# Rounding and subtracting the weights of a decoder layer in halves of eight k-tiles instead of quarters of four

## The chip, the cores and the metric

The kernel runs on one core of a Trainium2 chip. The metric is the device time of one execution in microseconds (us), shown as the median of three runs. One further execution was taken by the hardware profiler; all durations below are from it.

## What is computed

One layer of a decoder, for a prompt of 272 positions (16 learned tokens and 256 of the prompt) and for 64 sampled positions (8 requests of 8). Cut to what matters here:

```python
z = rmsnorm(x) @ w_in                    # split into q, k, v, indexer, conv, gate_A, gate_B
A = sparse_attend(q, k, v, top_k(index_scores(...))) @ w_attn_br
B = silu(layernorm(causal_conv(glu(cz)))) @ w_conv_br
h = x + (sigmoid(gate_A) * A + sigmoid(gate_B) * B) @ w_out
y = h + (silu(rmsnorm(h) @ w_gate) * (rmsnorm(h) @ w_up)) @ w_down
```

All of it is float32. The sampled positions read keys and values of 1024 earlier positions from a paged cache.

## The kernel before, in words

**Strips.** Every weight matrix goes through one pipeline, in strips of 128 output columns. A strip has 16 k-tiles of 128x128 (the fourth part of the feed-forward's last stretch, `dn2`, multiplies 12). SyncE loads a strip into one of four buffers, `RAW[:, s]`. ScalarE rounds it to the matmul's type, `WH` (two buffers, `s % 2`). VectorE writes the remainder `WL = RAW - WH` over `RAW`. TensorE makes three matmuls for each k-tile, `XH*WH + XL*WH + XH*WL` (L1355 to L1357), 48 for a strip, into the PSUM tile `G[s % 2]`; then VectorE or ScalarE reads it out.

**Who works for which strip.** While TensorE multiplies strip s, ScalarE and VectorE prepare strip s+2: `ahead` does a whole strip, `ahead_quarter` one piece of it at a time, between other work. Until now a piece is a quarter, 4 k-tiles. ScalarE's quarter r of strip s+2 overwrites the WH buffer of strip s, so it waits on `mm_done` until TensorE has multiplied quarter r of strip s (L535); VectorE's waits for ScalarE's on `hi_done` (L900); TensorE's matmuls wait on `lo_done`.

**The stage cz.** The GLU columns (16 strips, four loop passes of four) are multiplied while the paged keys come in. TensorE runs, for each quarter j of a strip (L1647 to L1671): eight transposes of one page of keys (`kst`) into PSUM, the 12 matmuls of the weight quarter j, and, on every second page, the 32 instructions of the scores `psS<-kTs,qsz` (16 matmuls in the code), which wait until both halves of that page have been copied from PSUM to `kTs`. ScalarE copies one half (L722) and VectorE the other (L1126); right after its copy number j, each calls `ahead_quarter(..., j)`. VectorE also has a top-k step (L1019 or L1023) behind its copies 0 and 2. So on both engines a copy and a weight piece alternate in one queue, and the order in which they stand there is the order of the code.

**Other stages that the prediction speaks of.** `qk` and `v` (projections, with `ahead`); the prompt's attention, which starts when VectorE has copied the last values; `ga` and `gbA` (gates), where VectorE alternates `ahead_quarter` with the depthwise convolution (L1205 and lines near it) and, at piece 14 of gbA's 16, makes `OL` (L1237), which the next stage's first matmul needs; `out`, whose last sum of squares TensorE takes at the end; and the three parts of the feed-forward, `gu` and `dn`.

Of the kernel before, what the change touches and what calls it, by code (L numbers as in the profile page):

```python
# [24 lines left out]
F32 = mybir.dt.float32  # L25
F32R = mybir.dt.float32r
I32 = mybir.dt.int32
ALU = mybir.AluOpType
ACT = mybir.ActivationFunctionType
# [12 lines left out]
IH, ID = 16, 64  # L42
# [184 lines left out]
def layer(nc, I, O):  # L227
# [34 lines left out]
    XH, XL, RAW, WH, WL = T["XH"], T["XL"], T["RAW"], T["WH"], T["WL"]  # L262
# [17 lines left out]
    nothing = zer[:, 0:4 * IH].rearrange("p (k n) -> p k n", k=4)  # L280
# [7 lines left out]
    with ExitStack() as ctx:  # L288
        G, TB, SB, MB = ([ctx.enter_context(nc.psum_tensor(f"ps{n}{i}", [P, 512], F32)) for i in range(2)] for n in "GTSM")

        def sem(name):
            return ctx.enter_context(nc.semaphore(name))
# [6 lines left out]
        hi_done, lo_done, mm_done = sem("hi_done"), sem("lo_done"), sem("mm_done")  # L299
# [225 lines left out]
        def _(act):  # L525
            ch = Chain(act, act_ch)

            def hi(G_, s, first=False):
                act.wait_ge(w_ld[s], 32 * G_ + 32)
                for r in range(4):  # L530
                    quarter(G_, s, r, first)

            def quarter(G_, s, r, first=False):
                if not first:
                    act.wait_ge(mm_done, 16 * G_ + (4 * s + r - 7))  # L535
                if isinstance(G_, int) and G_ == G0["ikiw"]:
                    if s:
                        act.activation(WH[:, s % 2, 4 * r:4 * r + 4, 0:IH], nothing, ACT.Copy).then_inc(hi_done, 1)
                        return
                    c = slice(0, ID + IH)  # L540
                else:
                    c = slice(0, P)
                act.activation(WH[:, s % 2, 4 * r:4 * r + 4, c], RAW[:, s, 4 * r:4 * r + 4, c], ACT.Copy).then_inc(hi_done, 1)  # L543

            def ahead(G_, s, last=False):
                if not (last and s >= 2):
# [2 lines left out]
            def ahead_quarter(G_, s, r):  # L549
                G_, s = G_ + (s + 2) // 4, (s + 2) % 4  # L550
                if r == 0:
                    act.wait_ge(w_ld[s], 32 * G_ + 32)
                quarter(G_, s, r)
# [62 lines left out]
            for i in range(2):  # L616
                c = slice(half * i, half * i + half)
                act.activation(ikT[0:ID, c], MB[0][0:ID, c], ACT.Copy).then_inc(ev[i], 1)
            for i in range(2):
                c = slice(half * i, half * i + half)  # L620
# [78 lines left out]
            for h in range(H):  # L699
                slot, c = h // 2 % 2, slice(P * (h % 2), P * (h % 2) + P)  # L700
# [188 lines left out]
        def _(dve):  # L889
# [4 lines left out]
            def lo(G_, s):  # L894
                for r in range(4):
                    quarter(G_, s, r)

            def quarter(G_, s, r):
                k = slice(4 * r, 4 * r + 4)
                dve.wait_ge(hi_done, 16 * G_ + (4 * s + r + 1))  # L900
                if isinstance(G_, int) and G_ == G0["ikiw"]:
                    if s:
                        dve.tensor_copy(WL[:, s, k, 0:IH], nothing).then_inc(lo_done, 1)
                        return
                    c = slice(0, ID + IH)
                else:
                    c = slice(0, P)
                dve.tensor_tensor(WL[:, s, k, c], RAW[:, s, k, c], WH[:, s % 2, k, c].bitcast(F32), ALU.subtract).then_inc(lo_done, 1)  # L908

            def ahead(G_, s, last=False):  # L910
                if not (last and s >= 2):
# [2 lines left out]
            def ahead_quarter(G_, s, r):  # L914
                quarter(G_ + (s + 2) // 4, (s + 2) % 4, r)
# [324 lines left out]
            for u in range(4 * GN["wa"]):  # L1240
                G_, s = G0["wa"] + u // 4, u % 4
# [32 lines left out]
            for u in range(4 * GN["wc"]):  # L1274
                G_, s, f = G0["wc"] + u // 4, u % 4, 2 * u
# [610 lines left out]
```

## Time and profile before

| | |
|---|---|
| median of three runs | 2174.16 us (2171.81 to 2174.58) |
| the profiled execution's own time | 2179.28 us |
| its span in the trace | 2177.8 us |
| TensorE (PE) matmuls | busy 2085.5 us, 96% of the span |
| VectorE (DVE) | busy 1235.7 us, 57% |
| ScalarE (ACT) | busy 902.6 us, 41% |
[...]

Busy time of TensorE is modelled from pipelined matmuls, so consecutive matmuls overlap in it: the distance between their starts tells the pace. "Idle before" is the time an engine waited ahead of an instruction, with what it waited for. [...]

### The profile page before, as it was taken

Reading aid. Unit: us, or ns where it says so; the run is one execution under the profiler, and the core shown is the slowest. Engines: PE = TensorE matmul, PEld = TensorE weight load, DVE = VectorE, ACT = ScalarE, POOL = GpSimd, SP = SyncE. Lnnn points to the kernel's source line nnn. Section 1 sums busy time; section 2 is a strip of 40 time slices with the busy share of each in tenths; the row PEclk is TensorE's granted clock in tenths of the full one; section 3 lists DMA queues with packets and bytes.
Section 4 is the critical chain, followed back from the end, with each engine's and each line's share of the span. In section 5 each row is a group of like instructions: output and inputs, shape, how many; then the busy total and the mean of one; then the engine's idle time right before and its main releaser. Section 6 shows DMA issues by size and latency. Waiting matters only on the chain.

```text
span 2177.8 us, 40501 instructions
## 1 busy us (share of the span) xinstructions
PE 2085.5 (96%) x14573; PEld 1970.8 (90%) x14573; DVE 1235.7 (57%) x2261; ACT 902.6 (41%) x1647; POOL 158.5 (7%) x286
## 2 busy tenths in 40 slices
PE   6969999979998999999999999999999999999997
PEld 5945999769997777999999999999999999999997
DVE  5324988526666799874664455554455544455553
ACT  6423443334444333436444454543344443344443
POOL 5300000011112121000000000000000000000012
PEclk9988999679998999999999999999999999999999
DMA  9450456237786798455654455555555555555574
GB/s 237 93 120 20 117 134 169 65 127 241 242 241 208 243 320 279 133 148 134 193 148 135 135 152 145 147 154 152 144 149 154 153 143 147 154 153 144 147 205 114
DMA packets 545493, 350.55 MB, mean 161 GB/s; under 512 B 15122, under 2 KB 524346, under 8 KB 545007
## 3 DMA queue, kind: packets, MB, share of 16 engines
q1 hardware_dynamic: 518480, 263.55, 44.9%
q0 software_dynamic: 25824, 84.55, 12.1%
q8 instruction: 70, 1.15, 0.2%
q10 hardware_dynamic: 1088, 1.05, 0.1%
q14 instruction: 31, 0.25, 0.0%
HBM read 338.91 MB, written 10.83 MB: 161 GB/s over the span
## 4 chain that ended last, share of the span: by engine, by line
PE 67%; DVE 1%; ACT 0%; issue 0%; POOL 0%; DVEq 0%; POOLq 0%; ACTq 0%
PE psG L1355 20%; PE psG L1356 20%; PE psG L1357 20%; PE psS L1352 2%; PE psM L1355 1%; PE psM L1356 1%; PE psM L1357 1%; PE psM L1352 1%; PE psM L1349 0%; PE psG L1349 0%; DVE stat L1178 0%; PE psT L1349 0%; DVE OL L1237 0%; ACT L L744 0%; PE psS L1349 0%
## 5 line engine op out<-in xcount | busy, mean ns | idle before, releaser
L908 DVE TENSOR_TENSOR WL<-RAW,WH 128x512 fp32r<-128x512 f32 (+1 forms) x996 | 672.6, 689 | 684.2 <-ACT WH L543 683.1
L543 ACT ACTIVATE WH<-RAW 128x512 fp32r<-128x512 f32 (+1 forms) x996 | 617.3, 629 | 886.7 <-PE psG L1357 827.2
L1355 PE MATMUL psG<-XH,WH 128*128 128x320 f32 (+1 forms) x2688 | 852.1, 317 | 19.7 <-ACT iwT L621 16.7
L1356 PE MATMUL psG<-XL,WH 128*128 128x320 f32 (+1 forms) x2688 | 841.8, 313 | 0.0
L1357 PE MATMUL psG<-XH,WL 128*128 128x320 f32 (+1 forms) x2688 | 839.6, 312 | 0.0
L1355 PEld LDWEIGHTS psG<-XH,WH 128*128 128x128 f32 x2688 | 510.3, 190 | 51.2 <-issue 30.9
L1356 PEld LDWEIGHTS psG<-XL,WH 128*128 128x128 f32 x2688 | 510.3, 190 | 1.1
L1357 PEld LDWEIGHTS psG<-XH,WL 128*128 128x128 f32 x2688 | 510.7, 190 | 0.0
L1355 PE MATMUL psG<-MH,WH 128*128 128x320 f32 x960 | 301.2, 314 | 0.3 <-DVE ML L1324 0.3
L1357 PE MATMUL psG<-MH,WL 128*128 128x320 f32 x960 | 296.6, 309 | 0.0
L1356 PE MATMUL psG<-ML,WH 128*128 128x320 f32 x960 | 296.5, 309 | 0.0
L1355 PEld LDWEIGHTS psG<-MH,WH 128*128 128x128 f32 x960 | 180.5, 188 | 1.6 <-issue 0.5
L1356 PEld LDWEIGHTS psG<-ML,WH 128*128 128x128 f32 x960 | 180.5, 188 | 1.1
L1357 PEld LDWEIGHTS psG<-MH,WL 128*128 128x128 f32 x960 | 180.4, 188 | 0.0
L1205 DVE SCALAR_TENSOR_TENSOR ya<-ub,wdw,ya 128x256 f32<-128x256 f32 x232 | 100.2, 479 | 0.0
L514 POOL DMA_DIRECT2D out<-ytok x16 | 11.5, 720 | 1101.7 <-ACT ytok L868 1097.7
L1349 PE MATMUL psT<-ident,kst 128*128 128x128 f32 x512 | 68.9, 278 | 6.2 <-DMA kst<-in_cache_k 6.2
L1349 PEld LDWEIGHTS psT<-ident,kst 128*128 128x128 f32 x512 | 58.0, 142 | 13.0 <-issue 12.5
L1126 DVE COPY kTs<-psT 128x512 f32<-128x512 f32 x64 | 43.9, 686 | 43.0 <-PE psT L1349 43.0
L722 ACT ACTIVATE kTs<-psT 128x512 f32<-128x512 f32 x64 | 38.2, 597 | 46.8 <-PE psT L1349 46.5
L858 ACT ACTIVATE MH<-at 128x320 f32 x44 | 20.8, 472 | 82.8 <-DVE at L1322 82.8
L480 POOL DMA_DIRECT2D kst<-in_cache_k x64 | 33.8, 529 | 176.7 <-issue 176.7
(347 smaller groups left out, 1729.7 us busy)
## 6 DMA issues: line engine op xcount, KB each, us to landing
RAW<-in_w_in SPq DMA_DIRECT2D x160, 512.0 KB, 5.2
RAW<-in_w_ffn_down SPq DMA_DIRECT2D x96, 512.0 KB, 5.0
RAW<-in_w_ffn_gate SPq DMA_DIRECT2D x88, 512.0 KB, 4.9
RAW<-in_w_ffn_up SPq DMA_DIRECT2D x88, 512.0 KB, 4.6
kst<-in_cache_k POOLq DMA_DIRECT2D x64, 512.0 KB, 4.5
vst<-in_cache_v POOLq DMA_DIRECT2D x64, 512.0 KB, 5.8
RAW<-in_w_out SPq DMA_DIRECT2D x32, 512.0 KB, 4.8
RAW<-in_w_attn_br SPq DMA_DIRECT2D x16, 512.0 KB, 4.7
```

Of the source, the lines that this page charges most:

```text
L480: pool.dma_start(dst[:, n:n + 1, :], src[bass.ds(page(g * m + n, ptab2), 1)].rearrange("o s n -> s o n")).then_inc(landed[n], 16)
L543: act.activation(WH[:, s % 2, 4 * r:4 * r + 4, c], RAW[:, s, 4 * r:4 * r + 4, c], ACT.Copy).then_inc(hi_done, 1)
L722: act.activation(kTs[:, j % 2, 0:4, :], TB[0][:].rearrange("p (h n) -> p h n", h=4), ACT.Copy).then_inc(kc_A, 1)
L858: act.activation(MH[:, bass.ds(g * 2 + s // 2, 1), :], at2[:, s // 2:s // 2 + 1, :], ACT.Copy).then_inc(ah_dn, 1)
L908: dve.tensor_tensor(WL[:, s, k, c], RAW[:, s, k, c], WH[:, s % 2, k, c].bitcast(F32), ALU.subtract).then_inc(lo_done, 1)
L1126: dve.tensor_copy(kTs[:, j % 2, 4:8, :], TB[1][:].rearrange("p (h n) -> p h n", h=4)).then_inc(kc_D, 1)
L1205: ch.step(dve.scalar_tensor_tensor(z, x, tap, z, ALU.mult, ALU.add))
L1349: return pe.transpose(out, src, ident[0:n, 0:n])
L1352: return pe.matmul(out, lhsT, rhs, start=start, stop=stop, skip_group_check=True)
L1355: pe.matmul(out, WH[:, s % 2, k], hi, start=start, stop=False)
L1356: pe.matmul(out, WH[:, s % 2, k], lo, start=False, stop=False)
L1357: return pe.matmul(out, WL[:, s, k], hi, start=False, stop=stop)
```

## The change

The pieces in which ScalarE rounds and VectorE subtracts become halves of 8 k-tiles. The calls stay where they were; those for odd pieces return at once. The call for piece 0 now does k-tiles 0 to 7 and waits for TensorE's quarters 0 and 1 of strip s; that for piece 2 does k-tiles 8 to 15 and waits for quarters 2 and 3. The counts on `hi_done` and `lo_done` go up by two at a time; TensorE's waits, the loads and all other work are as before.

```diff
@@ ScalarE @@
             def quarter(G_, s, r, first=False):
+                if r % 2:
+                    return
                 if not first:
-                    act.wait_ge(mm_done, 16 * G_ + (4 * s + r - 7))
+                    act.wait_ge(mm_done, 16 * G_ + (4 * s + r - 6))
...
-                act.activation(WH[:, s % 2, 4 * r:4 * r + 4, c], RAW[:, s, 4 * r:4 * r + 4, c], ACT.Copy).then_inc(hi_done, 1)
+                act.activation(WH[:, s % 2, 4 * r:4 * r + 8, c], RAW[:, s, 4 * r:4 * r + 8, c], ACT.Copy).then_inc(hi_done, 2)
@@ VectorE @@
             def quarter(G_, s, r):
-                k = slice(4 * r, 4 * r + 4)
-                dve.wait_ge(hi_done, 16 * G_ + (4 * s + r + 1))
+                if r % 2:
+                    return
+                k = slice(4 * r, 4 * r + 8)
+                dve.wait_ge(hi_done, 16 * G_ + (4 * s + r + 2))
...
-                dve.tensor_tensor(WL[:, s, k, c], RAW[:, s, k, c], WH[:, s % 2, k, c].bitcast(F32), ALU.subtract).then_inc(lo_done, 1)
+                dve.tensor_tensor(WL[:, s, k, c], RAW[:, s, k, c], WH[:, s % 2, k, c].bitcast(F32), ALU.subtract).then_inc(lo_done, 2)
```

ScalarE in the stage cz, from the first copy of a strip on (`kTs<-psT` is the copy of a page's half, `WH<-RAW` the rounding; names in brackets are the semaphores waited for). Before:

```order
L722 ACTIVATE kTs<-psT 128x512 [waits k_tr]
L552 ISA
L535 ISA [waits w_ld2]
L543 ACTIVATE WH<-RAW 128x512 [waits mm_done]
L721 REGISTER_ALU
L722 ACTIVATE kTs<-psT 128x512 [waits k_tr]
L535 REGISTER_ALU
L543 ACTIVATE WH<-RAW 128x512 [waits mm_done]
```

and with the change:

```order
L724 ACTIVATE kTs<-psT 128x512 [waits k_tr]
L554 ISA
L537 ISA [waits w_ld2]
L545 ACTIVATE WH<-RAW 128x1024 [waits mm_done]
L723 REGISTER_ALU
L724 ACTIVATE kTs<-psT 128x512 [waits k_tr]
L723 REGISTER_ALU
L724 ACTIVATE kTs<-psT 128x512 [waits k_tr]
```

The rounding of 1024 elements stands where that of 512 stood, between copy 0 and copy 1; behind copy 1 there is none any more. The order of the copies is the same, the `mm_done` that the rounding waits for is one quarter later.

VectorE in the same place (`WL<-RAW,WH` is the subtraction, `MAX` and `MATCH_REPLACE` the top-k step). Before:

```order
L1126 COPY kTs<-psT 128x512 [waits k_tr]
L104 ISA
L108 MEMSET stat 1x1 [waits dve_ch]
L1019 MAX m8s<-Ws 64x8
L900 ISA
L908 TENSOR_TENSOR WL<-RAW,WH 128x512 [waits hi_done]
L1125 REGISTER_ALU
L1126 COPY kTs<-psT 128x512 [waits k_tr]
L900 REGISTER_ALU
L908 TENSOR_TENSOR WL<-RAW,WH 128x512 [waits hi_done]
```

and with the change:

```order
L1130 COPY kTs<-psT 128x512 [waits k_tr]
L104 ISA
L108 MEMSET stat 1x1 [waits dve_ch]
L1023 MAX m8s<-Ws 64x8
L904 ISA
L912 TENSOR_TENSOR WL<-RAW,WH 128x1024 [waits hi_done]
L1129 REGISTER_ALU
L1130 COPY kTs<-psT 128x512 [waits k_tr]
L1129 REGISTER_ALU
L1130 COPY kTs<-psT 128x512 [waits k_tr]
```

As on ScalarE: copy 1 now stands behind a subtraction of a whole half.

VectorE at the end of gbA (`OL<-oT,OH` is the operand of the next stage's first matmuls, `ya` the convolution). Before:

```order
L908 TENSOR_TENSOR WL<-RAW,WH 128x512 [waits hi_done]
L1205 SCALAR_TENSOR_TENSOR ya<-ub,wdw,ya 128x256 [waits dve_ch]
L908 TENSOR_TENSOR WL<-RAW,WH 128x512 [waits hi_done]
L1237 TENSOR_TENSOR OL<-oT,OH 128x2560 [waits oh_dn]
L1205 SCALAR_TENSOR_TENSOR ya<-ub,wdw,ya 128x256 [waits dve_ch] x2
L908 TENSOR_TENSOR WL<-RAW,WH 128x512 [waits hi_done]
```

and with the change:

```order
L912 TENSOR_TENSOR WL<-RAW,WH 128x1024 [waits hi_done]
L1209 SCALAR_TENSOR_TENSOR ya<-ub,wdw,ya 128x256 [waits dve_ch] x2
L912 TENSOR_TENSOR WL<-RAW,WH 128x1024 [waits hi_done]
L1241 TENSOR_TENSOR OL<-oT,OH 128x2560 [waits oh_dn]
L1209 SCALAR_TENSOR_TENSOR ya<-ub,wdw,ya 128x256 [waits dve_ch] x3
L912 TENSOR_TENSOR WL<-RAW,WH 128x1024 [waits hi_done]
```

Before, one quarter of the strip came behind OL; now the whole strip's preparation comes ahead of it.

## Rows read from the trace of the kernel before

**Rows 1.** The page's busy time: us, share of the span, instructions.

```profile
PE 2085.5 (96%) x14573; PEld 1970.8 (90%) x14573; DVE 1235.7 (57%) x2261; ACT 902.6 (41%) x1647; POOL 158.5 (7%) x286
```

**Rows 2.** Stretches: us, busy (count) of PE, PEld, DVE, ACT, POOL; clock, DMA share, GB/s.

```profile
520.00:700.00 180.00, 173.46 (x1854) 160.62 (x1846) 112.37 (x205) 77.64 (x122) 30.34 (x58) 0.98 0.76 232
...
760.00:860.00 100.00, 100.00 (x687) 76.57 (x686) 92.66 (x183) 32.28 (x68) 20.71 (x39) 1.00 0.99 316
...
1500.00:1800.00 300.00, 300.00 (x2053) 300.00 (x2052) 148.81 (x247) 119.64 (x203) 0.00 (x0) 1.00 0.55 150
```

**Rows 3.** Groups of instructions by line and shape: count, busy us, mean ns, idle before.

```profile
L908 DVE TENSOR_TENSOR WL<-RAW,WH 128x512 fp32r<-128x512 f32 x992 | 670.7, 690 | 680.6 <-ACT WH L543 679.5 <-DVE rf L1306 0.2
L543 ACT ACTIVATE WH<-RAW 128x512 fp32r<-128x512 f32 x992 | 615.5, 629 | 883.0 <-PE psG L1357 823.5 <-PE psM L1357 28.8 <-DMA RAW<-in_w_in 14.3
...
L1237 DVE TENSOR_TENSOR OL<-oT,OH 128x2560 fp32r<-128x2560 f32 x1 | 2.8, 2819 | 0.0
...
L584 ACT ACTIVATE ikb<-ikst 128x1024 f32<-128x1024 f32 x8 | 8.5, 1061 | 0.2
```

**Rows 4.** Timeline of one page in cz: start us, us, engine, line, instruction, idle before.

```profile
569.61 1.04 PE L1349 MATMUL psT<-ident,kst 128*128 128x128 f32 x8
...
570.47 0.69 DVE L908 TENSOR_TENSOR WL<-RAW,WH 128x512 fp32r<-128x512 f32 x1 [0.68 <-ACT WH L543]
...
571.08 0.68 DVE L1126 COPY kTs<-psT 128x512 f32<-128x512 f32 x1
...
572.18 0.31 PE L1357 MATMUL psG<-XH,WL 128*128 128x336 f32 x1
572.42 1.08 PE L1352 MATMUL psS<-kTs,qsz 128*32 128x128 f32 x32
572.53 0.63 ACT L543 ACTIVATE WH<-RAW 128x512 fp32r<-128x512 f32 x1 [1.25 <-PE psG L1357]
573.19 0.69 DVE L908 TENSOR_TENSOR WL<-RAW,WH 128x512 fp32r<-128x512 f32 x1 [1.43 <-ACT WH L543]
```

**Rows 5.** Timeline at the end of gbA, around OL.

```profile
898.34 2.82 DVE L1237 TENSOR_TENSOR OL<-oT,OH 128x2560 fp32r<-128x2560 f32 x1
...
898.83 0.63 ACT L543 ACTIVATE WH<-RAW 128x512 fp32r<-128x512 f32 x1 [1.13 <-PE psG L1357]
...
901.30 0.38 PE L1355 MATMUL psG<-OH,WH 128*128 128x320 f32 x1 [2.52 <-DVE OL L1237]
```

**Rows 6.** What TensorE waited for: line, whom; us in total, times, longest.

```profile
PE psT L1352 <- DVE vs L1064: 2.2, 1, 2.2
PE psG L1355 <- DVE WL L908: 2.1, 1, 2.1
PE psM L1352 <- ACT sq L648: 2.0, 4, 0.5
PE psM L1352 <- ACT sq L840: 1.9, 1, 1.9
PE psM L1349 <- DVE L L1146: 1.8, 1, 1.8
...
PE psG L1355 <- DVE ML L1324: 0.3, 1, 0.3
```

**Rows 7.** Stretches behind four of TensorE's waits (columns as in rows 2).

```profile
36.00:40.00 4.00, 4.00 (x19) 4.00 (x18) 3.53 (x6) 2.12 (x5) 1.43 (x3) 0.57 1.01 353
...
689.00:692.00 3.00, 2.89 (x14) 1.98 (x12) 1.02 (x2) 1.84 (x4) 1.49 (x3) 0.55 0.88 259
900.00:904.00 4.00, 2.70 (x18) 2.73 (x19) 2.95 (x5) 0.60 (x1) 0.00 (x0) 1.00 0.94 257
1232.00:1236.00 4.00, 4.00 (x21) 4.00 (x21) 2.84 (x2) 2.26 (x3) 0.00 (x0) 0.70 0.07 18
```

**Rows 8.** Timeline of TensorE in the first of these stretches: matmuls 1 and 12.

```profile
36.48 0.47 PE L1355 MATMUL psG<-XH,WH 128*128 128x320 f32 x1
...
39.42 0.47 PE L1357 MATMUL psG<-XH,WL 128*128 128x320 f32 x1
```

More of the change, by code:

```diff
@@ L533, in quarter @@
             def quarter(G_, s, r, first=False):
+                if r % 2:
+                    return
                 if not first:
-                    act.wait_ge(mm_done, 16 * G_ + (4 * s + r - 7))
+                    act.wait_ge(mm_done, 16 * G_ + (4 * s + r - 6))
                 if isinstance(G_, int) and G_ == G0["ikiw"]:
                     if s:
-                        act.activation(WH[:, s % 2, 4 * r:4 * r + 4, 0:IH], nothing, ACT.Copy).then_inc(hi_done, 1)
+                        act.activation(WH[:, s % 2, 4 * r:4 * r + 4, 0:IH], nothing, ACT.Copy).then_inc(hi_done, 2)
                         return
@@ L898, in quarter @@
             def quarter(G_, s, r):
-                k = slice(4 * r, 4 * r + 4)
-                dve.wait_ge(hi_done, 16 * G_ + (4 * s + r + 1))
+                if r % 2:
+                    return
+                k = slice(4 * r, 4 * r + 8)
+                dve.wait_ge(hi_done, 16 * G_ + (4 * s + r + 2))
                 if isinstance(G_, int) and G_ == G0["ikiw"]:
                     if s:
-                        dve.tensor_copy(WL[:, s, k, 0:IH], nothing).then_inc(lo_done, 1)
+                        dve.tensor_copy(WL[:, s, 4 * r:4 * r + 4, 0:IH], nothing).then_inc(lo_done, 2)
                         return
```

## The prediction

> **What bounds the kernel now.** I read the page's busy times first, then the stretches, the groups of instructions by line, and the timeline of one page in the stage cz. TensorE is busy for 96% of the span [rows 1], and in the long weight stages it never stops: 2053 matmuls in 300 us, one every 0.146 us, at clock 1.00 [rows 2], so that a strip of 48 takes 7.0 us. ScalarE's rounding and VectorE's subtraction spend more time waiting than working: 883 us of idle ahead of 616 us of work, nearly all of it for TensorE's matmuls, and 681 us ahead of 671 us, nearly all of it for ScalarE [rows 3]. They are early, not late. So a saving on them is worth nothing by itself, and the question is where a later or longer piece makes TensorE wait.
>
> **What a piece costs.** A quarter takes 629 ns on ScalarE and 690 ns on VectorE [rows 3]. The halves have 1024 elements instead of 512. For ScalarE the group of ikb, a copy of 128x1024, shows 1061 ns: I take 1.06 us, 0.43 more than a quarter. For VectorE the subtraction of 2560 elements took 2819 ns [rows 3]; the line through 512 and 2560 gives 690 + 512 x (2819 - 690) / 2048 = 1222 ns, 0.53 more than a quarter. Two quarters cost 1258 and 1380 ns, so a strip saves 0.4 us on ScalarE and 0.3 us on VectorE, in time that they now spend waiting.
>
> **Steady strips: nothing.** The second half can start when TensorE ends strip s and is finished 1.06 + 1.22 us later, some 2.3 us; it is needed in the middle of strip s+2, 7.0 + 3.5 us later. PSUM is read out up to 0.96 us later than now, some 3 us after a strip's end, and needed again 7.0 us after it. That covers both.
>
> **The stage cz: a new wait on every second page.** Now, ScalarE's piece j waits for TensorE's quarter j, and while it is done TensorE is at the eight transposes and the matmuls of the next page; both copies of that page are finished long before TensorE asks for them. The timeline shows it: transposes from 569.61, VectorE's subtraction at 570.47, its copy at 571.08 to 571.76, TensorE's last matmul of the quarter at 572.18, and its scores at 572.42 without a wait [rows 4]. With the change piece 0 stands between copy 0 and copy 1, as before, but waits for TensorE's quarter 1, and that quarter is done only when TensorE stands in front of the scores that need copy 1. Copy 1 sits behind that piece on both engines. The same holds for piece 2 and copy 3. It is no deadlock, since quarter 1 doesn't need copy 1, but from then on everything is in series:
> - ScalarE starts at 572.53, as now [rows 4], and takes 1.06: 573.59.
> - VectorE starts 0.03 us after ScalarE's end (573.19 against 572.53 + 0.63 [rows 4]): 573.62. It takes 1.22: 574.84.
> - Its copy starts 0.08 us before the subtraction's shown end (571.08 against 570.47 + 0.69) and takes 0.68 [rows 4]: 574.76 to 575.44. ScalarE's own copy is ready sooner.
> - TensorE starts 0.14 us after VectorE's end (901.30 against 898.34 + 2.82 [rows 5]): 575.58.
>
> Against 572.42 that is 3.16 us of standstill, with nothing else for TensorE to do, since its instructions stand in order too. Two in each of 16 strips: 32 x 3.16 = **101 us**. What could be off by some tenths is each hand-over; I keep 2.9 and 3.4 us (93 and 109 us) as ends.
>
> [...]
>
> **The clock in cz.** Waits of this length have let TensorE's clock fall. Of four in the trace, 2.1 us for WL, 1.8 us for L, 1.9 us for sq at L840 [rows 6] and 2.5 us for OL [rows 5], the stretches behind the first three show a granted clock of 0.57, 0.55 and 0.70, the one behind OL 1.00 [rows 7]. [...] Between the two I take 1.25 us: 32 x 1.25 = **40 us**. The ends are nothing (the clock holds, as behind OL) and 60 us, if some of the slow stretches last longer than the one measured.
>
> **Single places where TensorE already waits for a piece or for what is behind one.** There the longer piece is paid in full, 0.43 us if only ScalarE's is in the chain and 0.96 us if both are:
> - at the start, for the first WL (2.1 us now): 0.96;
> - at the end of each pass of qk, for sq at L648 (four times, 0.5 each): 4 x 0.43 = 1.7;
> - at the start of the prompt's attention, for vs (2.2): 0.96;
> - at the end of out, for sq at L840 (1.9): 0.96;
> - at the start of the last dn, for ML (0.3): 0.96 [rows 6].
> - OL: it now starts at 898.34, behind a quarter that was ready early; with the change it comes behind the whole second half, which starts only at 898.83 [rows 5]: 898.83 + 1.06 + 0.03 + 1.22 - 0.08 = 901.06, so 2.7 us later, and TensorE waits 5.2 us instead of 2.5.
> - The end of cz: two quarters (0.63 + 0.69) are gone from behind TensorE's last quarter, ahead of the last logits; the last standstill has 1.3 us of this in it: minus 1.3.
>
> Together 7 us; I keep 3 and 11 as ends.
>
> **Stage ga.** From 760 to 860 VectorE is busy for 92.7% and TensorE for all of it [rows 2]. Its pieces may run late by up to a strip before TensorE notices, and halves make its work a little less. I take nothing.
>
> **The sum.** 101 + 40 + 7 = 148 us on the profiled execution's own 2179.28 us, 2327 us. That execution lies 5.1 us above the median of the runs, 2174.16 us, so the forecast for the median is **2322 us**, slower by 6.8%.
>
> **The rivals.**
> - *The clock holds in cz.* For it: behind OL it did [rows 7]. Against: three of four. 2174.2 + 101 + 7 = 2282 us. This lies inside the forecast's mechanism and its range; I don't count it apart.
> - *The clock stays low through all of cz.* Each standstill could come before the clock has recovered from the one ahead. For it: in cz as it is there are 180 us with the clock at 0.98 [rows 2], all of which could be lost. [...] Against: behind the waits shown the lower clock ends within some us of steady matmuls, and cz has over 6 us of them between two standstills. 0.08.
> - *Only one standstill in a strip, or half of each.* It would be so if one of the two copies weren't behind its piece after all. 2174.2 + 50 + 20 + 7 = 2251 us. Against: the order of both queues, which is the same at pieces 0 and 2. 0.03.
> - *Faster.* The pieces' fixed cost is what counts, in ga, where VectorE is busy for 92.7% [rows 2]: if TensorE there waited for WL, the change would give back 2 x 690 - 1222 = 158 ns twice in each of 16 strips, 5 us, and 2169 us if cz had no standstill. It decides from the point where VectorE runs behind by a whole strip; TensorE's busy time of 100.00 in that stretch says that it doesn't, and the series in cz is against it. [...] 0.03.
> - *No change.* The copies in cz are finished before TensorE asks, say because the pieces don't wait where I read it. 2174 us; 0.02.
>
> **How the numbers follow.** The forecast has 0.84. Its low end is 93 + 0 + 3 us on the median, 2270 us; its high end 109 + 60 + 11 us, 2354 us. I let the range reach to 2370 us, where part of cz would run at the lower clock throughout; beyond it lies the second rival, below it the third to fifth, together 0.16. A measurement of this kernel can tell a difference of about 0.2%, 4 us, from none. Faster by more than that: 0.03; within it: 0.02; slower by more: 0.95.
>
> **What would show it.** Right: in cz, TensorE's first scores instruction of every second page waits about 3.2 us for VectorE's kTs copy, 32 times, some 100 us in the list of waits; the pieces there stand in the timeline directly behind the last matmul of an odd quarter, with the copy directly behind the subtraction; half the pieces on both engines, of about 1.06 and 1.22 us; a granted clock well below 0.98 in cz; the wait for OL at 5.2 us. Wrong: if TensorE's idle time in cz stays small, the order isn't what I think; if the waits are there and the clock stays at 1.00, only the clock's term falls; if the kernel after cz takes clearly longer than before, I have missed a place.

## The result, and the profile after

The changed kernel takes **2362.8 us** (median of four runs, 2360.87 to 2364.72), the kernel before 2173.84 us beside it: a ratio of 1.0871 (1.0852 to 1.0890), 189 us more. The profiled execution took 2360.87 us, 181.6 us more than the profiled one of before (2179.28 us, which lies some 5 us above its median).

The page of the changed kernel, its busy times (columns as in [rows 1]):

```profile
PE 2153.2 (91%) x14573; PEld 2030.0 (86%) x14573; DVE 1179.7 (50%) x1757; ACT 814.6 (35%) x1143; POOL 159.0 (7%) x286
```

VectorE and ScalarE have 504 instructions less each and 56 and 88 us less to do. TensorE has the same 14573 matmuls and its share falls from 96% to 91%, because it now waits. Its granted clock in tenths of full speed, by slices of 59 us and from the same page, shows where:

```profile
PEclk9989998687777769999999999999999999999999
```

Slices 9 to 14 are from 472 to 826 us, most of the stage cz: one 8 and five times 7. What TensorE waited for, the rows that answer to [rows 6] and the new ones (line, whom; us in total, times, longest):

```profile
PE psS L1356 <- DVE kTs L1130: 83.9, 26, 3.2
PE psS L1356 <- issue: 19.1, 6, 3.2
...
PE psG L1359 <- DVE OL L1241: 5.4, 1, 5.4
...
PE psM L1356 <- ACT sq L650: 3.9, 4, 1.0
...
PE psG L1359 <- DVE SGA L1251: 3.4, 2, 1.7
...
PE psG L1359 <- DVE WL L912: 3.0, 1, 3.0
PE psM L1356 <- ACT sq L842: 3.0, 1, 3.0
PE psT L1356 <- DVE vs L1068: 2.8, 1, 2.8
...
PE psG L1359 <- DVE ML L1328: 1.4, 1, 1.4
```

The first two rows are new: 26 + 6 = 32 waits, 103.0 us in all, 3.2 us each, always ahead of the scores of a second page. ("issue" is the same wait where the profile saw no releaser.) The pieces themselves, groups by line and shape, answer to [rows 3]:

```profile
L912 DVE TENSOR_TENSOR WL<-RAW,WH 128x1024 fp32r<-128x1024 f32 x496 | 605.6, 1224 | 828.6 <-ACT WH L545 828.0 <-DVE Wp L1015 0.4
L545 ACT ACTIVATE WH<-RAW 128x1024 fp32r<-128x1024 f32 x496 | 523.9, 1059 | 972.4 <-PE psG L1361 914.5 <-PE psM L1361 32.6 <-issue 15.6
```

Half as many, of 1224 and 1059 ns, and both engines wait longer than before: what the larger pieces saved went into waiting.

The series itself, in the timeline of one page in cz (start us, us, engine, line, instruction, idle before), where [rows 4] had no wait:

```profile
622.31 0.31 PE L1361 MATMUL psG<-XH,WL 128*128 128x336 f32 x1
622.72 1.06 ACT L545 ACTIVATE WH<-RAW 128x1024 fp32r<-128x1024 f32 x1 [4.85 <-PE psG L1361]
...
623.88 1.23 DVE L912 TENSOR_TENSOR WL<-RAW,WH 128x1024 fp32r<-128x1024 f32 x1 [4.77 <-ACT WH L545]
625.02 0.68 DVE L1130 COPY kTs<-psT 128x512 f32<-128x512 f32 x1
...
625.80 1.93 PE L1356 MATMUL psS<-kTs,qsz 128*32 128x128 f32 x32 [3.18 <-issue]
...
627.67 1.78 PE L1353 MATMUL psT<-ident,kst 128*128 128x128 f32 x8
```

TensorE's last matmul of the quarter ends at 622.62; only then does ScalarE's rounding start, then the subtraction, then the copy, then the scores. And the scores take 1.93 us where they took 1.08: the standstill is followed by a slower clock, which is the other part of the loss.

Stretches of TensorE's clock, the columns of [rows 2] and the same two windows of 180 and 300 us, then the whole of cz:

```profile
520.00:700.00 180.00, 131.73 (x1083) 122.06 (x1082) 59.86 (x94) 38.82 (x53) 15.90 (x30) 0.78 0.43 130
...
1500.00:1800.00 300.00, 300.00 (x2049) 300.00 (x2048) 134.25 (x154) 115.88 (x123) 0.00 (x0) 1.00 0.54 148
...
476.00:852.00 376.00, 273.33 (x2265) 253.25 (x2263) 126.86 (x200) 80.64 (x111) 31.84 (x60) 0.80 0.43 130
```

In the same 180 us there are 1083 matmuls instead of 1854, at a granted clock of 0.78 instead of 0.98. (Before, cz ended at 686 us in this window: its part of it had a clock of 1.00, and the missing 0.02 belong to what comes behind cz.) In 300 us of the feed-forward there are 2049 against 2053, at 1.00: that stage noticed nothing. The kTs copies in cz begin at 474.0 and 683.6 us before, at 476.1 and 851.5 us now (first and last), so the stage went from 209.6 to 375.4 us. **165.8 of the 181.6 us are here**: 103.0 of standstill, and 62.8 that are left for the clock. The other 15.8 us lie outside cz.

### The profile page after: what moved, and what is told of

The parts are those of the page before. It is cut to its first block, busy times and chain, and to the rows that moved or that the text cites. A ratio compares the mean times of both kernels' runs of the same rounds, so it can differ in the third digit from the quotient of the medians.

```text
span 2359.4 us, 39696 instructions
## 1 busy us (share of the span) xinstructions
PE 2153.2 (91%) x14573; PEld 2030.0 (86%) x14573; DVE 1179.7 (50%) x1757; ACT 814.6 (35%) x1143; POOL 159.0 (7%) x286
## 4 chain that ended last, share of the span: by engine, by line
PE 61%; DVE 1%; ACT 1%; issue 0%; POOL 0%; DVEq 0%; POOLq 0%; ACTq 0%
PE psG L1359 19%; PE psG L1360 19%; PE psG L1361 19%; PE psS L1356 2%; PE psM L1360 1%; PE psM L1359 1%; PE psM L1356 1%; PE psM L1361 1%; ACT WH L545 0%; PE psM L1353 0%; DVE ub L1214 0%; DVE yp L1218 0%; PE psG L1353 0%; DVE stat L1182 0%; DVE WL L912 0%
## 5 line engine op out<-in xcount | busy, mean ns | idle before, releaser
L912 DVE TENSOR_TENSOR WL<-RAW,WH 128x1024 fp32r<-128x1024 f32 (+1 forms) x498 | 607.2, 1223 | 832.2 <-ACT WH L545 831.6
L1359 PE MATMUL psG<-XH,WH 128*128 128x320 f32 (+1 forms) x2688 | 860.9, 320 | 23.4 <-ACT iwT L623 17.7
L545 ACT ACTIVATE WH<-RAW 128x1024 fp32r<-128x1024 f32 (+1 forms) x498 | 525.4, 1057 | 976.2 <-PE psG L1361 918.3
L1359 PEld LDWEIGHTS psG<-XH,WH 128*128 128x128 f32 x2688 | 516.9, 192 | 55.0 <-issue 33.6
L1360 PEld LDWEIGHTS psG<-XL,WH 128*128 128x128 f32 x2688 | 516.2, 192 | 1.4 <-issue 0.4
L1356 PE MATMUL psS<-kTs,qsz 128*32 128x128 f32 x1024 | 60.6, 413 | 103.0 <-DVE kTs L1130 83.9
L1356 PEld LDWEIGHTS psS<-kTs,qsz 128*32 128x32 f32 x1024 | 47.2, 164 | 110.9 <-issue 110.9
L1353 PE MATMUL psT<-ident,kst 128*128 128x128 f32 x512 | 92.0, 340 | 6.0 <-DMA kst<-in_cache_k 6.0
L1353 PEld LDWEIGHTS psT<-ident,kst 128*128 128x128 f32 x512 | 78.7, 180 | 18.3 <-issue 17.9
```

Of the source, the lines that this page charges most:

```text
L545: act.activation(WH[:, s % 2, 4 * r:4 * r + 8, c], RAW[:, s, 4 * r:4 * r + 8, c], ACT.Copy).then_inc(hi_done, 2)
L1353: return pe.transpose(out, src, ident[0:n, 0:n])
L1356: return pe.matmul(out, lhsT, rhs, start=start, stop=stop, skip_group_check=True)
L1359: pe.matmul(out, WH[:, s % 2, k], hi, start=start, stop=False)
L1360: pe.matmul(out, WH[:, s % 2, k], lo, start=False, stop=False)
```

## The experiments

Theory: the 32 standstills come from the order in the two queues (the piece behind copy 0 waits for TensorE's next quarter, copy 1 stands behind the piece), and the low clock comes from the standstills. Rivals: the size of the pieces as such is what costs, the low clock has a cause of its own in cz, or a good part of the loss lies outside cz. The first four runs shared a chip and nine runs of the kernel before (2172.51 us); the last four another chip and 21 runs of it (2172.59 us).

### Halves everywhere but in cz

ScalarE's and VectorE's old functions for a quarter are kept beside the new ones, under the name `fourth`, and cz calls them:

```diff
-                        ahead_quarter(G0["cz"] + g, s, j)
+                        ahead_fourth(G0["cz"] + g, s, j)
@@ VectorE @@
-                        ahead_quarter(G_, s, j)
+                        ahead_fourth(G_, s, j)
```

> Halves everywhere except in the stage cz, where the pieces are quarters again. Theory A (the order in cz: a half stands ahead of the copy that TensorE waits for, and its signal comes a quarter later): the 103 us of standstill and the low clock behind them are gone; cz is as long as before (210 us) and what is left is the small places outside cz, 10 to 16 us, so 2184 to 2190 us. Rival B (larger pieces cost wherever they are, by crowding the engines or the memory): most of the 189 us stays, over 2300 us.

Measured: 2190.98 us, ratio 1.0086 (1.0061 to 1.0112). The stretch of cz in this kernel:

```profile
474.00:685.00 211.00, 211.00 (x2267) 197.75 (x2265) 130.15 (x231) 89.77 (x142) 31.69 (x60) 1.00 0.74 230
```

Clock 1.00, TensorE busy throughout, no wait for kTs in the list, and cz 209.2 us long as before. So of 189 us about 171 belong to cz. What is left, 18.5 us, is well over the prediction's 7 us for the single places (3 to 11), and a little more than the 10 to 16 us that I expected of this run. Its list of waits has OL at 5.4 us and a row that the prediction doesn't name:

```profile
PE psG L1392 <- DVE OL L1274: 5.4, 1, 5.4
...
PE psG L1392 <- DVE SGA L1284: 3.4, 2, 1.7
```

### Quarters everywhere but in cz

The reverse: the kernel before, with halves in cz alone (`ahead_half` is the change's function under a name of its own).

```diff
-                        ahead_quarter(G0["cz"] + g, s, j)
+                        ahead_half(G0["cz"] + g, s, j)
@@ VectorE @@
-                        ahead_quarter(G_, s, j)
+                        ahead_half(G_, s, j)
```

> Quarters everywhere except in the stage cz, where the pieces are halves. Theory A: 32 waits of 3.2 us and a granted clock of about 0.8 in cz, 2174 + 166 = 2340 us (2335 to 2346). Rival B: only cz's share of the pieces (32 of 496 halves), so below 2200 us.

Measured: 2342.9 us, ratio 1.0782 (1.0734 to 1.0829). Its waits and its stretch of cz:

```profile
PE psS L1389 <- DVE kTs L1163: 83.9, 26, 3.2
PE psS L1389 <- issue: 19.1, 6, 3.2
...
PE psG L1392 <- DVE OL L1274: 2.5, 1, 2.5
```

```profile
471.00:845.00 374.00, 270.97 (x2266) 251.12 (x2269) 126.79 (x202) 80.00 (x111) 31.69 (x60) 0.80 0.43 130
```

The same 103.0 us and the same clock of 0.80; OL is back at 2.5 us. The two halves of the change add up: 170.4 + 18.5 = 188.9 us, against 189.0 measured for both together.

### The half called behind the odd copy

Halves everywhere as in the change, but in cz piece 0 is called behind copy 1 and piece 2 behind copy 3, so that no copy stands behind a piece that waits for the quarter in front of that copy's scores.

```diff
-                        ahead_quarter(G0["cz"] + g, s, j)
+                        if j % 2:
+                            ahead_quarter(G0["cz"] + g, s, j - 1)
@@ VectorE @@
-                        ahead_quarter(G_, s, j)
+                        if j % 2:
+                            ahead_quarter(G_, s, j - 1)
```

> Halves everywhere, but in cz both engines do piece 0 behind copy 1 and piece 2 behind copy 3, in place of behind copies 0 and 2. The size of the pieces and the signals they wait for stay the same. Theory A (place in the queue): nothing that TensorE waits for stands behind a waiting piece any longer; the 32 waits fall to less than 0.3 us each, the clock in cz is back above 0.97, and the time is that of cz in quarters, 2184 to 2196 us (VectorE has the logits of two pages to do behind piece 2, which may cost up to 5 us). Rival C (the later signal itself: the weights are prepared a quarter later and that is what TensorE feels): over 2300 us still.

Measured: 2199.09 us, ratio 1.0113 (1.0073 to 1.0153), 3 us above the upper end. The 32 waits of the scores are gone. What TensorE still waits for kTs, and the stretch of cz:

```profile
PE psT L1355 <- DVE kTs L1131: 3.5, 7, 0.5
```

```profile
476.00:690.00 214.00, 210.46 (x2251) 195.68 (x2251) 124.59 (x198) 82.23 (x109) 31.69 (x60) 0.99 0.74 227
```

The pieces are as large as in the change, and 164 of the 189 us are gone: size alone is not the cause, order is. The kernel takes 8.1 us more than with cz in quarters. Of these, 4.8 us are in cz: 3.5 us are waits of the transposes for a PSUM buffer that VectorE's copy releases, a copy that now stands behind a half. The other 1.3 us in cz and the 3.3 us outside it aren't assigned.

### The standstill filled with matmuls that lead to nothing

The change, with 20 matmuls of 128x320 put ahead of the scores of every second page. They write to PSUM that nobody reads and wait for nobody, so TensorE is active through the standstill; 640 more matmuls in all. (The first added line waits once, ahead of cz, until ScalarE has read out what stood in that PSUM tile.)

```diff
+            pe.wait_ge(sc_cp, CT)
...
+                        if n % 2:
+                            for _ in range(20):
+                                mm(MB[0][:, 0:NQ], XH[:, 0, 0:P], XH[:, 0, 0:NQ])
```

> The changed kernel with 20 matmuls of 128x320 that lead to nothing in each of the 32 standstills (ahead of the wait for copies 1 and 3), about 3 us each at the full clock; it computes nothing else than before. Theory D (64 of cz's 167 us are TensorE's lower clock behind the standstills): the waits themselves shrink to 0.2 to 0.4 us because the filling takes their place, cz is no shorter by that, but its clock goes to 0.97 or more and it loses about 60 us: 2300 us (2295 to 2312). Rival E (transposes and scores run slower for another reason, say the transfers of keys and weights beside them): no less than 2355 us.

Measured: **2297.38 us**, ratio 1.0574 (1.0534 to 1.0614): with 640 matmuls more, 65 us less than the changed kernel. Its waits for kTs, and its stretch of cz:

```profile
PE psS L1356 <- DVE kTs L1130: 7.9, 26, 0.3
...
PE psS L1356 <- issue: 1.6, 6, 0.3
```

```profile
478.00:792.00 314.00, 304.81 (x2897) 290.65 (x2895) 125.07 (x197) 80.20 (x110) 31.13 (x59) 1.00 0.50 153
```

The clock is 1.00 and every one of the scores takes 1.08 us. Cz is 105.9 us longer than before: the standstill of 103 us is all there, the clock's part is gone. So the low clock follows from TensorE standing still. Its price of 62.8 us, until now only what was left over, is measured by itself: 60 us between cz's first and last copy (375.4 to 315.5 us), 65 us by the medians of the two kernels.

### Quarters that wait as late as the halves

The kernel before, with quarter-sized pieces; in cz pieces 0 and 1 stand together behind copy 0 and wait for TensorE's quarter 1, as the half does (2 and 3 likewise).

```diff
-                        ahead_quarter(G0["cz"] + g, s, j)
+                        if j % 2 == 0:
+                            n_, t_ = G0["cz"] + g + (s + 2) // 4, (s + 2) % 4
+                            act.wait_ge(mm_done, 16 * n_ + (4 * t_ + j - 6))
+                            for r in (j, j + 1):
+                                ahead_quarter(G0["cz"] + g, s, r)
@@ VectorE @@
-                        ahead_quarter(G_, s, j)
+                        if j % 2 == 0:
+                            for r in (j, j + 1):
+                                ahead_quarter(G_, s, r)
```

> The kernel before with one difference in cz: behind copy 0 both engines do pieces 0 and 1, behind copy 2 pieces 2 and 3, still quarters of four k-tiles, and ScalarE first waits for the later signal, as the halves do. Theory A (the place and the signal, not the size of an instruction): the 32 standstills are there, shorter by what the two engines overlap. Quarters behind one another end at 0.66 + 0.61 + 0.69 = 1.96 us after TensorE's last matmul instead of 2.35 us, so 2.8 us each, 90 us, and on top 30 to 60 us of lower clock: 2290 to 2325 us. Rival F (the size of the piece): no more than 0.4 us each, below 2190 us.

Measured: 2299.37 us, ratio 1.0569 (1.0536 to 1.0603). Small pieces, and most of the loss is there: 126.8 of the 170.4 us that halves in cz alone cost come with the later signal. Its waits and its clock in cz:

```profile
PE psS L1358 <- DVE kTs L1130: 73.4, 26, 2.9
...
PE psS L1358 <- issue: 17.1, 6, 2.9
```

```profile
472.00:803.00 331.00, 241.62 (x2266) 223.88 (x2265) 128.21 (x231) 83.46 (x143) 31.70 (x60) 0.90 0.48 147
```

The wait is shorter, 90.5 us / 32 = 2.8 us, since VectorE begins the first quarter (at 606.85 us in one of them) while ScalarE does the second (both from 606.19 to 607.34). Cz is 121.2 us longer, so only 30.7 us are the clock's, half of the 62.8. So the size of the piece does count, by the length of the standstill: 12.5 us less of waiting, and with the shorter standstills 32.1 us less of lower clock. The timeline of TensorE shows where the clock's part went, in two standstills in a row:

```profile
608.85 1.94 PE L1358 MATMUL psS<-kTs,qsz 128*32 128x128 f32 x32 [2.85 <-issue]
...
619.80 1.08 PE L1358 MATMUL psS<-kTs,qsz 128*32 128x128 f32 x32 [2.82 <-DVE kTs L1130]
```

and the clock granted behind each:

```profile
608.85:612.16 3.31, 3.31 (x41) 2.93 (x41) 0.00 (x0) 0.00 (x0) 0.00 (x0) 0.53 0.00 0
619.80:622.60 2.80, 2.80 (x46) 2.60 (x47) 0.66 (x3) 0.60 (x1) 0.00 (x0) 1.00 1.17 313
```

Behind one wait of 2.8 us the granted clock is 0.53, behind the next, as long, 1.00. From 527 us on they alternate without exception; in all of cz the scores are slowed behind 17 of the 32 standstills (two of them in part), and behind the first only the transposes are, which makes 18. In the changed kernel, with 3.2 us, the scores are slowed behind 31 of 32 (one in part). A standstill with a slow clock behind it costs 30.7 / 18 = 1.7 us here and 62.8 / 31 = 2.0 us there: what differs most is how often it falls due.

### The gates in quarters as well

The first experiment, with quarters also in gbA and wa on both engines, and on ScalarE in gbB. This goes after the waits outside cz. (`ahead_fourths` calls `ahead_fourth` for all four quarters.)

```diff
-                ahead_quarter(G0["gbA"], n // 4, n % 4)
+                ahead_fourth(G0["gbA"], n // 4, n % 4)
@@ VectorE, wa @@
-                    ahead_quarter(G_, s, r)
+                    ahead_fourth(G_, s, r)
@@ ScalarE, gb (in wa the same) @@
-                ahead(G_, s)
+                ahead_fourths(G_, s)
```

> Quarters in cz, in the gates gbA (on ScalarE also in gbB) and in wa; halves elsewhere. What is tried is the cost of halves in gbA and wa, beside the kernel with only cz in quarters (2191.0 us). Theory G: the later OL (2.9 us of wait and 1.5 us of lower clock behind it) and the two waits for SGA in wa (3.4 us), which I had left out, are due to a whole half and two lots of convolution standing ahead of them: 7 to 8 us less, 2183 us, OL's wait back at 2.5 us and no wait for SGA. Rival H (convolution steps run late whatever the pieces): no change, 2191 us.

Measured: 2184.66 us, ratio 1.0055 (1.0033 to 1.0077), 6.3 us less than with cz alone in quarters. OL is back at 2.5 us and there is no wait for SGA:

```profile
PE psG L1396 <- DVE OL L1278: 2.5, 1, 2.5
```

2.9 us for OL and 3.4 for SGA are 6.3 us. That this fits to a tenth is luck: the theory had 1.5 us more, for the lower clock behind OL, and the runs of each of the two kernels spread over 4 to 5 us. The two sets of runs don't overlap (2180.24 to 2185.09 against 2189.19 to 2193.07).

### OL made earlier, in the first experiment and in the kernel before

With cz in quarters and halves elsewhere, OL is made at piece 9 of gbA instead of 14; then the same edit alone, in the kernel before.

```diff
-                if n == 14:
+                if n == 9:
                     dve.wait_ge(oh_dn, 1)
```

> As the kernel with only cz in quarters (2191.0 us), but VectorE makes OL five pieces earlier, behind piece 9 of gbA instead of piece 14. Theory G: the wait for OL (5.4 us) and the lower clock behind it (1.5 us) are gone; the waits for SGA stay, as they hang on the convolution steps: 2184 us. Rival I: OL's 2.8 us on VectorE only move, and TensorE waits somewhere else in wa as much longer: 2189 us or more.

Measured: 2183.57 us, ratio 1.0047 (1.0028 to 1.0066), 7.4 us less than with OL late. No wait for OL is left, and SGA's stays:

```profile
PE psG L1392 <- DVE SGA L1284: 3.4, 2, 1.7
```

The wait was 5.4 us. The other 2 us fit the clock that was lost behind it (at most 1.7 us, as the section below shows), but a difference of that size is not clear of the spread of the runs.

> The kernel before with OL made behind piece 9 of gbA instead of piece 14, nothing else. The wait of 2.5 us for OL is gone and no other comes: 2.5 us less than before, 0.1%, about what a measurement can just tell. Rival: VectorE is busy there and the convolution moves back: no change.

Measured: 2171.47 us (12 runs) against 2172.59, ratio 0.9998 (0.9978 to 1.0017). In the trace the wait of 2.5 us is gone, but 2.5 us are 0.1%, and the runs spread from 2158 to 2178 us: by time this is undecided. No version here is shown to beat the kernel before.

## Why the prediction was right, and where its sizes were off

The forecast was 2322 us, slower, with a range of 2270 to 2370; 2362.8 lies inside, 41 us above the point, and the mechanism is the one forecast. The sizes were less good: the upper ends of its own terms add up to 2354, and only the widening to 2370 holds the result. Of the 41 us, 23 are the clock in cz, 9 the single places and 2 the standstills; the other 7 are scatter, since the profiled execution of before lay 5 us above its median and that of the changed kernel 2 us below.

- **The standstills: right.** 32 were forecast at 3.16 us, 101 us; 32 came at 3.2, 103.0 us, at the place and in the order that the steps gave. With halves but no copy behind the late signal they are gone (half called later), with quarters behind the late signal they are there (late quarters): it is the signal and the queue that make them; the size only sets how long they last.
- **The clock in cz: the step that was mis-sized.** The prediction took 1.25 us a standstill, 40 us; it was 2.0 us, 63 us, above even its upper end of 60. No run shows the 1.25 us, a value that I chose between two estimates: twelve weight matmuls at the lower level behind WL, 0.267 us apart [rows 8] in place of 0.146, are 12 x 0.121 = 1.45 us, and three quarters of that are 1.1. The weighing was a little low: 31 of 32 had the lower clock, where three of four waits had shown it before [rows 7], and 1.45 us for each would have given 46 us. The larger part is the length. The cost of a fall was read from that one stretch, 3.2 us of weight matmuls. In cz the scores and eight transposes follow the standstill, and behind every second one the lower level lasts longer than that, into the weight matmuls:

```profile
613.40:616.90 3.50, 3.50 (x41) 3.12 (x41) 1.08 (x3) 0.00 (x0) 0.00 (x0) 0.50 0.88 229
616.90:622.60 5.70, 5.70 (x34) 5.43 (x32) 1.84 (x3) 0.60 (x1) 1.06 (x2) 0.82 0.32 92
625.80:629.20 3.40, 3.40 (x40) 3.02 (x41) 0.00 (x0) 0.00 (x0) 0.00 (x0) 0.51 0.00 0
629.20:634.00 4.80, 4.80 (x35) 4.55 (x33) 1.90 (x4) 0.60 (x1) 1.06 (x2) 1.00 0.35 108
```

  Two standstills in a row of the changed kernel, ended at 613.40 and 625.80: both have about 0.50 up to the end of the transposes; behind the first the weight matmuls run at 0.82, behind the second at 1.00. That is some 5.5 us at the lower level behind the first (3.5 us, and twice 0.18 x 5.7) and 3.4 us behind the second. What runs there matters little: the weight matmuls lost 0.121 of 0.267 us each, 45%, the scores lose 1.93 - 1.08 = 0.85 us, 44%, the transposes of the page shown 1.78 - 1.04 = 0.74 us, 42%. 45% of 5.5 and of 3.4 us are 2.5 and 1.5 us, 2.0 on average, the price that was measured. The prediction had this case, slow stretches longer than the one measured, as the end of its range and not as its point. Why the lower level lasts longer behind every second standstill is not shown.
- **Single places: 7 us forecast, 15.8 in the traces, 18.5 by the runs.** The waits that were named came out close: OL 5.4 (forecast 5.2), WL 3.0 (2.1 + 0.96), sq at the end of out 3.0 (1.9 + 0.96), vs 2.8 (2.2 + 0.96), ML 1.4 (0.3 + 0.96), and sq in qk 3.9 (2.0 + 1.7). The 1.3 us forecast as a gain at the end of cz didn't come: the stretch from cz's last scores to ga's first matmul is 1.2 us longer than before (28.9 against 27.7 us). The wait for the logits `L` there did fall, but only by 0.6 us, to 1.2, and the last scores alone lost 0.86 us to the clock. Two things were missed. One is the clock behind OL: it was 1.00 there before [rows 7], and now is 0.81 over the 9 us that follow,

```profile
1071.00:1080.00 9.00, 6.84 (x37) 6.87 (x38) 3.60 (x5) 1.06 (x1) 0.00 (x0) 0.81 0.23 60
```

  at most 9 x 0.19 = 1.7 us. The other is SGA, 3.4 us. In wa VectorE does its second half only when the strip has ended, and two lots of convolution then stand ahead of the two readings of PSUM that TensorE waits for, as the timeline of both engines there shows:

```profile
1090.15 1.23 DVE L912 TENSOR_TENSOR WL<-RAW,WH 128x1024 fp32r<-128x1024 f32 x1 [1.08 <-ACT WH L545]
1091.29 1.19 DVE L1218 TENSOR_TENSOR yp<-ub,wdw 128x992 f32<-128x992 f32 x1
...
1094.96 1.19 DVE L1214 TENSOR_REDUCE ub<-yp 128x32 f32<-128x992 f32 x1
...
1096.69 0.48 DVE L1250 TENSOR_TENSOR SGA<-psG,SGA 128x320 f32<-128x320 f32 x1
1097.09 0.48 DVE L1251 TENSOR_TENSOR SGA<-psM,SGA 128x320 f32<-128x320 f32 x1
...
1097.62 0.42 PE L1359 MATMUL psG<-OH,WH 128*128 128x320 f32 x1 [1.70 <-DVE SGA L1251]
```

  The step "Steady strips: nothing" failed here. It counted the piece and the reading of PSUM as following each other directly; in wa other work lies between them. Not all of the 18.5 us is assigned: with the gates in quarters 12.1 us are left (7.2 to 16.7). Against the profile of before, the named waits in that run's trace make some 5.6 us of it (sq 1.9 and 1.1, ML 1.1, WL 0.9, vs 0.6); how the rest is shared between the lower clock behind them and scatter stays open.
- **Steady strips elsewhere, and ga: right.** The feed-forward keeps its pace, and the pieces measured 1224 and 1059 ns against 1222 and 1060 forecast.
- **The rivals.** That the clock holds is excluded by 0.80 in cz; that it stays low through all of it by the 1.00 from 629.20 on. The result, 2362.8 us, lies between the 2282 us of the first and the 2422 us that I had worked out for the second (140 us for the clock: 93 us for 768 weight matmuls, each 0.121 us longer, the rest an estimate for transposes and scores). Faster or no change is excluded by every run with halves in cz. The size of the pieces: in cz, smaller ones went with the shorter time (2363 us with the half, 2191 with quarters in cz). But 2199 us with halves called later and 2299 with late quarters show that here it is mainly the signal waited for, and what is queued behind it, that decide.

## What to carry to other kernels

Merging two pieces of work doesn't just make one longer piece: it waits for the later of the two signals, and whatever stands behind it in the same queue waits with it. So for each merged piece look at what is queued behind it and who needs that before the later signal can come; here this cost 103 us, and no saving on two idle engines could pay for it. Price the clock that a standstill loses by how long the lower level lasts behind that standstill, and not by the stretch behind another wait: here it was 3.4 and 5.5 us in turn, against the 3.2 us that had been read elsewhere.

## What the runs showed of the hardware that was not expected

- 640 useless matmuls in the standstills made the kernel 65 us faster, since the clock stayed at 1.00 instead of 0.80.
- Two waits of 2.8 us in the same place of the same loop were followed by a granted clock of 0.53 once and of 1.00 the next time, in turn; at 3.2 us the scores were slowed behind 31 of 32. With 0.4 us more of waiting the clock's loss in cz was twice as large, 63 us instead of 31. A single wait in a trace didn't tell what a repeated one would do, nor even the same one in another run: behind the wait of 2.5 us for OL, whose code is the same in both, the clock over the next 9 us was 1.00 in the kernel before and 0.81 with the late quarters:

```profile
901.30:910.30 9.00, 9.00 (x61) 9.00 (x62) 6.32 (x14) 2.53 (x4) 0.00 (x0) 1.00 0.36 99
...
1021.17:1030.17 9.00, 9.00 (x51) 9.00 (x52) 5.30 (x11) 2.04 (x4) 0.00 (x0) 0.81 0.33 91
```
